# Projection weights of a decoder step: twelve loads of 768 columns through two buffers, instead of eighteen of 512 through three

## What is computed

```python
def project_qkv(u, w_qkv, q_gain, k_gain):
    b, t, _ = u.shape
    z = jnp.einsum('btd,df->btf', u, w_qkv).reshape(b, t, N_DGROUPS, 3, N_HEADS, HEAD_DIM)
    q = rms_norm(z[:, :, :, 0], q_gain[:, None, :])
    k = rms_norm(z[:, :, :, 1], k_gain[:, None, :])
    return q, k, z[:, :, :, 2]
```

## Time and profile before

| | |
|---|---|
| median of 3 runs | 1264.16 us (1261.74 to 1264.27) |
| profiled execution, its own time | 1266.1 us |
| its span (first to last instruction) | 1263.9 us |
| PE busy | 1113.8 us (88%) |
| mean granted TensorE clock | 0.922 of full |
| bytes moved by the DMA engines | 462.63 MB, 366 GB/s over the span |
| the projection's matmuls (L1059) | 30.3 to 351.0 us, 276.0 us busy |

### The profile page before, as it was taken

One profiled execution on the slowest core, in us unless ns is written; L12 is line 12 of the kernel. 1 busy time (PEld: TensorE's weight loads), 2 busy tenths in 40 slices (PEclk: granted clock), 3 DMA queues, 4 the chain that ended last, 5 costly groups with the idle time before them and its releaser, 6 DMA issues.

```text
span 1263.9 us, 15314 instructions
## 1 busy us (share of the span) xinstructions
PE 1113.8 (88%) x4993; PEld 671.7 (53%) x4994; DVE 435.8 (34%) x859; ACT 234.0 (19%) x524; POOL 225.0 (18%) x484
## 2 busy tenths in 40 slices
PE   5998799999949899974979999999464999999998
PEld 3887588788822588863424444434343344334444
DVE  3456455845830366223101111111743111111113
ACT  1121122112110134211112122111101112112210
POOL 1014112411420122002122222110001122222210
PEclk9999899999967699985989999999665999999999
DMA  9999999999879998899999999999999899999996
GB/s 374 334 357 372 385 387 343 369 389 388 322 239 384 368 308 288 344 320 326 330 399 429 430 427 413 400 399 394 399 325 322 327 396 397 398 395 396 409 420 241
DMA packets 62930, 462.63 MB, mean 366 GB/s; under 512 B 12112, under 2 KB 20192, under 8 KB 47888
## 3 DMA queue, kind: packets, MB, share of 16 engines
q1 hardware_dynamic: 49136, 440.29, 90.8%
q0 software_dynamic: 5536, 18.88, 4.1%
q10 hardware_dynamic: 8232, 3.13, 1.1%
HBM read 455.19 MB, written 183.41 MB: 505 GB/s over the span
## 4 chain that ended last, share of the span: by engine, by line
PE 56%; DVE 8%; DMA 4%; issue 3%; POOL 1%; ACT 1%; ACTq 1%; POOLq 0%; DVEq 0%; SPq 0%
PE bank L1242 17%; PE bank L1264 8%; PE bank L1220 7%; PE bank L1209 5%; DMA region_a<-in_w_up_dram 3%; PE bank L1171 2%; PE bank L1103 2%; PE bank L1130 1%; PE bank L287 1%; PE bank L1138 1%; PE bank L1150 1%; PE bank L1181 1%; PE bank L1270 1%; PE bank L1110 1%; PE bank L1127 1%
## 5 line engine op out<-in xcount | busy, mean ns | idle before, releaser
L1059 PE MATMUL bank<-uT,ring_lo 128*128 128x264 f32 x1152 | 276.0, 394 | 8.5 <-DVE uT L300 6.0
L1059 PEld LDWEIGHTS bank<-uT,ring_lo 128*128 128x128 f32 x1152 | 219.5, 195 | 49.4 <-issue 9.7
L1242 PE MATMUL bank<-ring_lo,scratch 128*64 128x512 f32 x512 | 114.7, 601 | 16.0 <-DMA ring_lo<-in_w_gate_dram 8.0
L787 DVE RECIPROCAL scratch<-scratch 128x264 f32<-128x264 f32 x48 | 86.5, 1802 | 111.0 <-ACT scratch L632 111.0
L1220 PE MATMUL bank<-scratch 128*128 128x512 f32 (+1 forms) x192 | 99.7, 646 | 18.0 <-POOL scratch L570 18.0
L1264 PE MATMUL bank<-ring_lo,scratch 128*64 128x512 f32 x512 | 113.4, 595 | 1.3 <-issue 1.3
L1242 PE MATMUL bank<-region_a,scratch 128*64 128x512 f32 x512 | 112.7, 592 | 1.4 <-DMA region_a<-in_w_up_dram 1.4
L966 DVE TENSOR_TENSOR scratch<-bank,scratch 128x512 f32<-128x512 f32 x16 | 11.1, 691 | 228.5 <-PE bank L1242 228.5
L1209 PE MATMUL bank<-scratch 128*128 128x264 f32 x288 | 80.1, 404 | 4.4 <-DVE scratch L966 3.4
L555 POOL TENSOR_TENSOR small<-epsc 128x1 f32<-128x1 f32 x83 | 15.6, 193 | 378.7 <-PE bank L1270 359.9
L1242 PEld LDWEIGHTS bank<-ring_lo,scratch 128*64 128x64 f32 x512 | 36.8, 138 | 83.6 <-issue 75.4
(11 more groups left out here) (224 smaller groups left out, 1242.4 us busy)
## 6 DMA issues: line engine op xcount, KB each, us to landing
out_dram<-in_cache_kv_w_dram SPq DMA_DIRECT2D x128, 1023.5 KB, 18.8
ring_lo<-in_w_gate_dram SPq DMA_DIRECT2D x32, 2048.0 KB, 12.0
region_a<-in_w_up_dram SPq DMA_DIRECT2D x32, 2048.0 KB, 15.2
ring_lo<-in_w_down_dram SPq DMA_DIRECT2D x32, 2048.0 KB, 16.5
ring_lo<-in_w_qkv_dram SPq DMA_DIRECT2D x18, 2048.0 KB, 18.0
out_dram<-in_cache_kv_w_dram SPq DMA_DIRECT2D x32, 1022.0 KB, 35.9
ring_lo<-in_cache_kv_w_dram POOLq DMA_DIRECT2D x24, 512.0 KB, 11.8
ring_lo<-in_cache_kv_w_dram SPq DMA_DIRECT2D x6, 2048.0 KB, 14.7
```

What stands on the lines that cost most here:

```text
L787: chain(vec.reciprocal(zri[:, n % 2, :], zr[:, n % 2, :]))
L1059: last = mm(z_bank[s % 4][:, 0:T], w[:, k, at:at + P], uT[:, k, :], start=(k == 0), stop=(k == KT - 1))
L1242: last = mm(bank[2 + w][rows, :], u_slots[:, k, rows], weights[e][w][:, k, :], start=(k == 0), stop=(k == KT - 1))
```

## The change

The projection's weights come in chunks of `QC` = 768 columns, 8 pieces of 3 KB on each partition, 3 MB in all, into two buffers `qkv_buffer(0)` and `qkv_buffer(1)`, which together take the place of slots 0 to 2. A chunk feeds `QPC` = 6 tiles. SP issues two chunks at the start and then two in each of five rounds, each behind the wait for the tiles that used its buffer, with five copies behind each. The buffers have semaphores of their own, so the counts on `ring_full` start from 0 (`RING_KV`). The values' loads at the end of the stage wait for other tiles: slot 0 lies in buffer 0, slots 1 and 2 overlap buffer 1.

```diff
+    QC = 768
+    QPC = QC // P
+    CHUNKS = G * NZ // QPC
...
+        def qkv_buffer(c):
+            return ring_lo[:, c * KT * QC:(c + 1) * KT * QC].rearrange("p (k n) -> p k n", k=KT)
...
-        RING_KV = CHUNKS // 3
+        RING_KV = 0
...
-            for c in range(3):
-                sp.dma_start(slot(c).rearrange("p (k n) -> p k n", k=KT), qkv_chunks[c]).then_inc(ring_full[c], 16)
+            for c in range(2):
+                sp.dma_start(qkv_buffer(c), qkv_chunks[c]).then_inc(qkv_full[c], 16)
...
-            with sp.Fori(1, CHUNKS // 3) as r:
-                for c in range(3):
-                    sp.wait_ge(z_ready, r * (3 * TPC) + (c - 2) * TPC)
-                    sp.dma_start(slot(c).rearrange("p (k n) -> p k n", k=KT),
-                                 qkv_chunks[ds(r * 3 + c, 1)].rearrange("a p k n -> p (a k) n")).then_inc(ring_full[c], 16)
-                    for n in range(3 * c, 3 * c + 3 + c // 2):
+            with sp.Fori(1, CHUNKS // 2) as r:
+                for c in range(2):
+                    sp.wait_ge(z_ready, r * (2 * QPC) + (c - 1) * QPC)
+                    sp.dma_start(qkv_buffer(c), qkv_chunks[ds(r * 2 + c, 1)].rearrange("a p k n -> p (a k) n")).then_inc(qkv_full[c], 16)
+                    for n in range(5 * c, 5 * c + 5):
                         move(2, r, n)
...
-                        sp.wait_ge(z_ready, G * NZ - (2 - g) * TPC)
+                        sp.wait_ge(z_ready, G * NZ - (QPC if g == 0 else 0))
...
-                        c = s // TPC
-                        if s % TPC == 0:
-                            pe.wait_ge(ring_full[c % 3], g * 32 + 16 * (c // 3 + 1))
+                        c = s // QPC
+                        if s % QPC == 0:
+                            pe.wait_ge(qkv_full[c % 2], g * 32 + 16 * (c // 2 + 1))
...
-                        w = slot(c % 3).rearrange("p (k n) -> p k n", k=KT)
-                        at = s % TPC * P
+                        w = qkv_buffer(c % 2)
+                        at = s % QPC * P
```

More of the change, by code:

```diff
@@ L71, in build @@
     NQK = 2 * KT
-    CHUNKS = G * NZ // TPC
+    QC = 768
+    QPC = QC // P
+    CHUNKS = G * NZ // QPC
     caches = (cache_w128, cache_w512, cache_w2048)
@@ L78, in build @@
     MAX_ROUNDS = LAYERS * NP * -(-T // CAP)
-    assert SEQ == 2 * P and BH == P and KT * P == D and LAYERS == 2 and NZ // TPC == 6
+    assert SEQ == 2 * P and BH == P and KT * P == D and LAYERS == 2 and NZ // QPC == 4
     qkvs_dram = nc.dram_tensor("qkv_of_samples", [NS, 3, G, D], F32, kind="Internal").ap()
@@ L222, in build @@
         ring_full = [sem(f"ring_full{n}") for n in range(6)]
+        qkv_full = [sem(f"qkv_full{n}") for n in range(2)]
         dve_own, pool_own = sem("dve_own"), sem("pool_own")
@@ L271, in build @@
         SENT_PER_G = 4
-        RING_KV = CHUNKS // 3
+        RING_KV = 0
         RING_WO = RING_KV + 2
-        qkv_chunks = w_qkv[0].rearrange("(k p) (c n) -> c p k n", p=P, n=CW)
+        qkv_chunks = w_qkv[0].rearrange("(k p) (c n) -> c p k n", p=P, n=QC)
         k_strided = [c[0].rearrange("b (s d) w h e -> b w s d (h e)", d=d)[:, 0, :, 0, :] for c, d in zip(caches, DILATIONS)]
```

## The result

The changed kernel takes **1290.74 us** (median of 4 runs, 1286.98 to 1295.81) against 1264.22 for the kernel before on the same chip (4 runs, 1261.74 to 1264.92): a ratio of 1.022, with a 95% interval of 1.018 to 1.026. It is 26.5 us slower. The profiled execution has a span of 1286.6 us against 1263.9, so 22.7 us are there to be found.

A forecast was written before the change was run, and what follows sets the result against it. It took the kernel to be near two limits, DMA engines nearly always busy and a projection paced by PE and DVE's scoring. Terms -3.5 - 1 - 1 + 5.5 = 0 gave 1264.2 us, range 1256 to 1272.

The forecast's parts named there:

- What bounds the kernel: Projection: paced by PE within a group and DVE's scoring at group ends, DMA engines nearly always busy, weight chunks hidden.
- the lead of a chunk: Projection refills: requested 6 tiles ahead instead of 8, still landing in time; 0 us, upper end 4 us.
- rival (b): Late weights in the projection: two or three refills late cost 8 to 12 us, 1274 us; chance 0.12.
- The start and the 3 KB pieces: Projection: PE starts on `uT`, not weights, and larger pieces bring no difference in rate; 0 us each.
- (d): SP's queue: six fewer transfers free it sooner if each has a fixed time; 11 us, 1253 us; chance 0.04.
- Group 0's keys: End of group 0: key loads of samples 4 to 6 meet a chunk, not copies; 3.5 us saved.
- Group 1's keys: End of group 1: no term of its own; its loads' 5.7 to 7.7 us served as yardstick for group 0.
- q rows and stores of group 1: Moves of q rows in groups 1 and 2, and group 1's stores beside a chunk; 1 us saved each.
- rival (c): Gains at keys, q rows and stores come whole, the end-of-stage jam costs only 2.3 us; 1256.7 us; chance 0.24.
- The end of the stage: After the projection: values' loads and a copy, issued together, delay the chain's small transfers; 5.5 us lost, bounds 1 and 12.
- Rival (a): End of the stage: a jam of 8 us there with only 1 saved elsewhere, 1271 us; chance 0.17.
- Behind it: After the stage: whatever PE gains or loses is carried on, since the transfer-bound stretch starts at PE's time.

The follow-up runs named there:

- e7: The changed kernel without the fifty cache copies of the loop, so not all work is done: 1261.27 us, 0.997.
- e8: The kernel before without the same fifty cache copies of the loop: 1251.71 us, 0.989.
- e2: The kernel before with an edit meant to cut copies into 16 KB pieces; pieces were rejoined, so it is the same kernel: 1261.81 us, 1.000.
- e9: The changed kernel with its copies handed over in threes and fours at the tile counts of the kernel before: 1281.12 us, 1.015.
- e10: The changed kernel with copies dealt to its ten refills as 6, 6, 0, 6, 7, 5, 0, 6, 8, 6: 1273.79 us, 1.011.
- e3: The kernel before with each round's ten copies as five, five and none behind its three chunks: 1270.92 us, 1.007.
- e13: The changed kernel with copies dealt to its ten refills as 8, 8, 0, 1, 9, 8, 0, 2, 8, 6: 1281.67 us, 1.017.
- e6: The kernel before with only the changed kernel's waits for the values' loads (66, 72 and 72 tiles): 1269.15 us, 1.004.
- e1: The changed kernel with an edit meant to cut copies into 16 KB pieces; pieces were rejoined, so it is the same kernel: 1285.66 us, 1.018.
- e17: The changed kernel with cache copies truly broken into 8 KB pieces, eight to a row: 1428.86 us, 1.126.
- e15: The changed kernel with cache copies truly broken into 16 KB pieces, four to a row: 1275.17 us, 1.011.

## Why the prediction was wrong, point by point

- **What bounds the kernel, and the lead of a chunk: right.** Refills 1 to 3 were to land at 77.3, 99.8 and 122.7 us. They were issued at 58.35, 83.06 and 109.07 and took 19.4, 17.1 and 13.1: 77.8, 100.2 and 122.2. Each was issued 1.8 us later than forecast, so that all three agree to half a microsecond is in part luck. PE never waits for weights, so rival (b) did not happen. The start and the 3 KB pieces cost nothing that can be seen; (d) is out by e7 against e8. The 12 us that the prediction worked out from the Trainium skill, "DMA: Bandwidth & Descriptors", Anatomy of one DMA, are not seen either; the 2 us are fitted there on transfers issued by POOL.
- **Group 0's keys: the step that failed.** It said that the keys of samples 4 to 6 would come beside a chunk, in 5.7 to 7.7 us. They were issued from 118.8 us, and the chunk was through at 122.2. But no packet of POOL's queue moved in those microseconds. This is what started to move from 118 to 123 us, all of it on SP's queue:

```profile
DMA packets 276, 2.57 MB, mean 514 GB/s; under 512 B 29, under 2 KB 29, under 8 KB 247
...
q1 hardware_dynamic: 276, 2.57, 126.4%
```

  The first key packet started at 123.2, 4.4 us after its issue, when the chunk was gone. Behind it stood five copies, which landed one after the other from 124.9 to 138.8, and all four loads took 15.8 to 19.8 us. The mistake was to ask what lies in SP's queue when a load is issued. What counts is what lies in it from the load's first packet, here 4 us later, until it has landed; and the chunk was not stretched to 126 us, since no key packet shared with it. Forecast -3.5, measured +6.5 (+8.8 against the 4.1 us of the twin e2), within the bound of 9.8 lost that the step itself named.
- **Group 1's keys: the step that was missing.** Their 5.7 to 7.7 us were used as a yardstick for group 0 and never asked what becomes of them. Two things moved. The refill there now waits for 42 tiles instead of 44. Before, the keys were requested from 227.4 us, ahead of the chunk issued at 231.3, and had all landed at 242.3, ahead of that chunk (243.9) and of the three copies behind it. Now they were requested from 235.5, behind the chunk issued at 231.7, which landed at 244.9, and the loads of samples 6 and 7 met its five copies and took 21.0 and 20.3 us. Measured +11.7, forecast 0: the largest term. That copies are the cause is shown by e7 (none, 5.9 to 8.3 us), e9 and e10 (none behind that chunk while the loads are in flight, 7.4 to 9.0) and, from the other side, e3 and e13. How much is the place of the run and how much its length was not tried apart.
- **q rows and stores of group 1: right and small.** Forecast -1 and -1, measured -1.7 and -0.9. (They are the only part of rival (c), "gains whole, the jam small", that came.)
- **The end of the stage: right.** Forecast +5.5, measured +6.8; alone in e6 +6.7. Rival (a), "jam at the stage's end alone", had the sign but not the size, since the jam was a quarter of the loss.
- **Behind it: right.** What PE lost in the projection was carried to the end to within 2 us.

With -3.5 replaced by +6.5 and +11.7 added, the same sum gives 1264.2 + 10 + 11.7 = 1285.9 us, against 1290.74 measured, and 1285.66 in e1, the same kernel. No rival had either key term: (a) let group 0 save less, and the bound of 9.8 us lost went into none of them.

## What to carry to other kernels

When bulk copies share a queue with paced loads, what counts for a third party on another queue is the run of copies that is moving while its transfer is in flight, by length and by place. A long run where nobody else loads costs less than a shorter one beside a load: e10 has runs of up to eight, and is 10 us or more faster than the changed kernel with its runs of five. Fewer, larger loads lengthen the runs and move them to other tiles, even if bytes and rates are unchanged. Follow every customer of the other queues, at every group's end and not only where there was a wait before: here key loads, then the stores, became late in turn as the copies were moved about. And look at the packet count of a run before believing that an edit of a transfer did anything.

## What the hardware showed that was not expected

Copies in pieces of 8 KB slow the kernel by 150 us against pieces of 16 KB, and not evenly. The page of e17 and that of the changed kernel, on the copies with 1023.5 KB and with 1022.0 KB each:

```profile
out_dram<-in_cache_kv_w_dram SPq DMA_DIRECT2D x128, 1023.5 KB, 21.8
...
out_dram<-in_cache_kv_w_dram SPq DMA_DIRECT2D x32, 1022.0 KB, 61.8
```

```profile
out_dram<-in_cache_kv_w_dram SPq DMA_DIRECT2D x128, 1023.5 KB, 19.1
...
out_dram<-in_cache_kv_w_dram SPq DMA_DIRECT2D x32, 1022.0 KB, 34.1
```

Only the second kind is much slower. Its pieces are 8176 bytes, those of the first kind 8188. In the packet records of e17 the mean piece of 8176 bytes took 928 ns, that of 8188 bytes 390, and that of 8128 bytes, in the eight copies of the smallest cache, 377. The stretch from 630 to 760 us of e17, and then of the changed kernel (PE, PEld, DVE, ACT, POOL, PEclk, DMA share, GB/s):

```profile
630.00:760.00 130.00, 23.07 (x112) 20.29 (x112) 17.00 (x68) 7.21 (x9) 0.00 (x0) 0.54 1.05 134
```

```profile
630.00:760.00 130.00, 117.86 (x499) 48.13 (x497) 19.45 (x41) 21.46 (x30) 23.48 (x64) 0.97 1.00 403
```

The engines are as busy and move a third of the bytes, 134 against 403 GB/s. At 16 KB the same copies showed nothing of it (35.0 us in e15). Why a piece of 8176 bytes is slow where one of 8188 is not was not tried.
